# First modulation weight of a decoder layer taken in four slices of channels, with x and the weight rows between them

## What is computed

```python
mod = jax.nn.silu(c) @ w_ada[l] + b_ada[l]                        # (1, 6 * 1024)
sh1, sc1, g1, sh2, sc2, g2 = [m[:, None, :] for m in jnp.split(mod, 6, axis=-1)]
u = x * (1.0 + sc1) + sh1
proj = u @ w_in                                                   # q, k and v are 1536 of its columns
```

## Time and profile before

| | |
|---|---|
| median of 3 runs | 2779.15 us (2772.14 to 2779.37) |
| the profiled execution, its own time | 2779.9 us |
| its span | 2777.3 us |
| mean granted TensorE clock | 0.953 |
| TensorE busy with matmuls | 2509.4 us, 90% |
| VectorE, ScalarE, GpSimd busy | 53%, 40%, 30% |

### The profile page before, as it was taken

The page is one execution under the profiler, slowest core; times in us unless marked ns, Lnnn a source line. Parts: engine busy times, 40 slices in busy tenths (PEclk is TensorE's granted clock), DMA queues, the critical chain, the costliest instruction groups (busy, mean ns, idle before and its releaser), DMA issues. The chain is left out here.

```text
span 2777.3 us, 36162 instructions
## 1 busy us (share of the span) xinstructions
PE 2509.4 (90%) x12525; PEld 2093.1 (75%) x12526; DVE 1485.0 (53%) x1928; ACT 1114.9 (40%) x1819; POOL 829.5 (30%) x707
## 2 busy tenths in 40 slices
PE   5999899999999999999989969894998999999970
PEld 4788678778888888888878858774887888887850
DVE  6222155665665656665653356666547445526636
ACT  3122144554454545454530021112547546526633
POOL 2111022442222222222212235565232223222336
PEclk9999899999999999999999989996999999999985
DMA  7699666767666675766447546423558656627726
GB/s 260 236 315 321 239 211 185 247 199 233 193 213 185 212 216 177 218 211 198 156 152 247 167 153 229 144 99 122 166 154 286 179 151 189 202 62 224 252 68 242
DMA packets 258781, 549.61 MB, mean 198 GB/s; under 512 B 23860, under 2 KB 93608, under 8 KB 258024
## 3 DMA queue, kind: packets, MB, share of 16 engines
q1 hardware_dynamic: 236072, 483.07, 52.5%
q0 software_dynamic: 15248, 46.62, 7.6%
q10 hardware_dynamic: 7344, 18.35, 1.7%
HBM read 394.94 MB, written 153.02 MB: 197 GB/s over the span
## 5 line engine op out<-in xcount | busy, mean ns | idle before, releaser
L93 PE MATMUL mx_acc<-u_u,mx_w_hi 128*128 128x512 f32 x1792 | 572.8, 401 | 2.5 <-DMA mx_w_lo<-halves 2.5
L722 POOL TENSOR_TENSOR mx_wt<-mx_wt,mx_rest 128x127 f32<-128x127 f32 (+15 forms) x128 | 271.5, 2121 | 741.4 <-DVE mx_rest L924 741.4
L93 PEld LDWEIGHTS mx_acc<-u_u,mx_w_hi 128*128 128x128 f32 x1792 | 326.8, 190 | 68.2 <-DMA mx_w_lo<-halves 4.0
L932 DVE TENSOR_TENSOR mx_wt_lo<-mx_p_t,mx_wt_hi 128x512 fp32r<-128x512 f32 (+2 forms) x320 | 192.2, 605 | 331.2 <-ACT mx_wt_hi L887 329.4
L93 PE MATMUL mx_acc<-u_u,mx_w_lo 128*128 128x512 f32 x896 | 353.6, 395 | 0.0
L887 ACT ACTIVATE mx_wt_hi<-mx_p_t 128x512 fp32r<-128x512 f32 (+2 forms) x320 | 171.0, 534 | 408.5 <-PE mx_p_t L774 362.4
L924 DVE TENSOR_TENSOR_SCAN mx_rest<-mx_rest,mx_zero 128x128 f32<-128x128 f32 (+15 forms) x128 | 315.0, 2461 | 9.1 <-ACT mx_wt L869 9.1
L93 PE MATMUL moe_p_gu<-keep_wide_hi,moe_x_hi 128*128 128x512 f32 x656 | 262.6, 400 | 13.5 <-DVE keep_wide_lo L1916 13.0
L93 PE MATMUL moe_p_gu<-keep_wide_hi,moe_x_lo 128*128 128x512 f32 x656 | 257.8, 393 | 0.0
L93 PE MATMUL moe_p_gu<-keep_wide_lo,moe_x_hi 128*128 128x512 f32 x656 | 257.6, 393 | 0.0
L868 ACT ACTIVATE mx_rest<-mx_p_z 128x512 f32<-128x512 f32 (+2 forms) x320 | 171.1, 535 | 99.5 <-PE mx_p_z L761 59.2
(11 more groups left out here) (250 smaller groups left out, 5177.9 us busy)
## 6 DMA issues: line engine op xcount, KB each, us to landing
mx_w_hi<-halves SPq DMA_DIRECT2D x98, 512.0 KB, 3.8
mx_w_lo<-halves SPq DMA_DIRECT2D x98, 512.0 KB, 5.3
keep_stay<-in_w_gate SPq DMA_DIRECT2D x64, 512.0 KB, 5.2
keep_stay<-in_w_up SPq DMA_DIRECT2D x64, 512.0 KB, 6.2
keep_stay<-in_w_down SPq DMA_DIRECT2D x32, 1024.0 KB, 6.8
u_saved<-u_u SPq DMA_DIRECT2D x4, 4096.0 KB, 19.5
mx_w_mod<-in_w_ada SPq DMA_DIRECT2D x64, 256.0 KB, 5.2
gate_t<-mx_g_out SPq DMA_DIRECT2D x64, 256.0 KB, 5.2
```

The source lines that it names most:

```text
L93: mm = pe.matmul(out, a, b, start=first and n == 0, stop=last and n == len(pairs) - 1, skip_group_check=True)
L722: pool.tensor_tensor(wt[:, t % 2, 0:w - 1], wt[:, t % 2, 0:w - 1], rest[:, t % 2, 1:w], ALU.mult).then_inc(m["weights_done"], 1)
L932: dve.tensor_tensor(wt_lo[:, first:first + k - j], p_t[:, n % TR, 0:(k - j) * P].rearrange("p (j t) -> p j t", t=P), f32(wt_hi[:, first:fi ...
```

## The change

`w_ada` is no longer taken by halves but by four slices of channels: slice i holds the shift and the scale of channels 256 i to 256 i + 255, which is what u's row chunks k = 2i and 2i + 1 need. A slice is 2 MB, loaded by eight DMAs of 128 x 2 x 256 (rows of 1 KB, where they were 4 KB) into half of the second half of `stay`. SP's order becomes: slice 0, x, weight rows 0 and 1, slice 1, rows 2 and 3, slice 2, rows 4 and 5, slice 3, rows 6 to 15. Slice i waits until slice i - 2 has been summed up. VectorE sums a slice with one tensor_scalar and seven scalar_tensor_tensor of 512 channels, each of which waits for the one before it; TensorE then sums over partitions with four matmuls, and VectorE adds them to `mod`. ScalarE's affine of chunk k waits for its slice's step. These sums now stand inside the k loop, ahead of chunks 0, 2, 4 and 6. `p_t` has three buffers (a PSUM bank goes to `p_mod`). In the k loop TensorE's transposes of chunk k + 3 come behind the products of chunk k.

```diff
-    MW = FIRST_MOD * NB
-    AB, TR = 4, 4
+    AB, TR = 4, 3
-    MH, WH = MW // 2, QW // 2
+    WH = QW // 2
+    SLICES = 4
+    SC = D // SLICES
+    SK = KD // SLICES
...
-        ring = s.sb("ring", [P, RS, MH])
+        ring = s.sb("ring", [P, RS, D])
+        ada = flat(stay, 1).rearrange("p (b k h n) -> p b k h n", b=2, k=KD, h=2)
...
-            for n in range(2 * KD):
-                k, half = divmod(n, 2)
-
-                past(sp, m["summed"], n - RS + 1)
-                sp.dma_start(ring[:, n % RS], ada_view[:, k, half * MH:(half + 1) * MH]).then_inc(ring_in[n % RS], 16)
+
+            def load_slice(i):
+                past(sp, m["summed"], KD * (i - 1))
+                for q in range(SLICES):
+                    for h in range(2):
+                        sp.dma_start(ada[:, i % 2, SK * q:SK * (q + 1), h], ada_view[:, SK * q:SK * (q + 1), h * D + i * SC:h * D + (i + 1) * SC]
+                                     ).then_inc(ada_in[i % 2][q], 16)
+
+            def load_w(n):
+                half, k = divmod(n, KD)
+                past(sp, m["w_lo_done"], n - RS + 1)
+                sp.dma_start(ring[:, n % RS, 0:WH], in_view[:, k, c_q + half * WH:c_q + (half + 1) * WH]
+                             ).then_inc(ring_in[n % RS], 16)
+
+            load_slice(0)
             sp.dma_start(xr[:], x_view[:, 0]).then_inc(m["x_in"], 16)
             for n in range(2 * KD):
-                half, k = divmod(n, KD)
-                if n < RS:
-                    sp.wait_ge(m["summed"], 2 * KD - RS + n + 1)
-                else:
-                    sp.wait_ge(m["w_lo_done"], n - RS + 1)
-                sp.dma_start(ring[:, n % RS, 0:WH], in_view[:, k, c_q + half * WH:c_q + (half + 1) * WH]
-                             ).then_inc(ring_in[n % RS], 16)
+                if n < KD and n > 0 and n % SK == 0:
+                    load_slice(n // SK)
+                load_w(n)
...
-            for j in range(FIRST_COLS):
-                half, a = divmod(j * P, MH)
-                if a == 0:
-                    pe.wait_ge(m["summed"], 2 * KD - 1 + half)
-                mm = pe.matmul(p_mod[:, j:j + 1], msum[:, half, a:a + P], one[:], start=True, stop=True,
-                               skip_group_check=True)
-            mm.then_inc(m["mod_summed"], 1)
+            def sum_rows(i):
+                pe.wait_ge(m["summed"], KD * (i + 1))
+                for h in range(2):
+                    for j in range(SK):
+                        n = h * KD + i * SK + j
+                        mm = pe.matmul(p_mod[:, n:n + 1], msum[:, i, h, j * P:(j + 1) * P], one[:], start=True, stop=True,
+                                       skip_group_check=True)
+                mm.then_inc(m["mod_summed"], 1)
+
+            sum_rows(0)
             for k in range(TR):
                 turn(0, k)
             pe.wait_ge(m["cols_out"], 2)
             for k in range(KD):
+                pe.wait_ge(m["u_lo_done"], k + 1)
+                pe.wait_ge(m["w_lo_done"], k + 1)
+                for i in range(AB):
+                    part(0, i, k)
+                if (k + 1) % SK == 0 and k + 1 < KD:
+                    sum_rows((k + 1) // SK)
                 if TR + k < KD:
                     turn(0, TR + k)
-                pe.wait_ge(m["u_lo_done"], k + 1)
-                pe.wait_ge(m["w_lo_done"], k + 1)
-                if k == 0:
-                    pe.wait_ge(m["mod_step"], 1)
-                for i in range(AB):
-                    part(0, i, k)
...
-            act.wait_ge(m["mod_step"], 2)
             for k in range(KD):
+                act.wait_ge(m["mod_step"], k // SK + 2)
                 affine(0, k)
                 high_w(k)
...
+            def sum_slice(i):
+                for k in range(KD):
+                    dve.wait_ge(ada_in[i % 2][k // SK], 32 * (i // 2 + 1))
+                    if k == 0:
+                        ins = dve.tensor_scalar(msum[:, i], ada[:, i % 2, 0], csilu[:, 0:1], None, ALU.mult)
+                    else:
+                        dve.wait_ge(m["summed"], KD * i + k)
+                        ins = dve.scalar_tensor_tensor(out=msum[:, i], in0=ada[:, i % 2, k], scalar=csilu[:, k:k + 1],
+                                                       in1=msum[:, i], op0=ALU.mult, op1=ALU.add)
+                    ins.then_inc(m["summed"], 1)
+                dve.wait_ge(m["mod_summed"], i + 1)
+                dve.wait_ge(m["mod_step"], i + 1)
+                cols, sums = (v.rearrange("p (h k) -> p h k", h=2)[:, :, SK * i:SK * (i + 1)]
+                              for v in (mod[:, 0:FIRST_COLS], p_mod[:, 0:FIRST_COLS]))
+                dve.tensor_tensor(cols, cols, sums, ALU.add).then_inc(m["mod_step"], 1)
...
             for k in range(KD):
+                if k % SK == 0:
+                    sum_slice(k // SK)
                 high(0, k)
                 low_w(k)
```

More of the change, by code:

```diff
@@ L137, in load_piece, with front @@
             bass.ds(e, 1), :, a - KD:b - KD].rearrange("e p k d -> p (e k) d")).then_inc(piece_in[i], 16)
-def front(nc, used, keep, x, c, w_ada, b_ada, w_conv, w_in, u, u_in, u_saved, qk_hi, qk_lo, v_tok, halves):
+def front(nc, used, keep, stay, x, c, w_ada, b_ada, w_conv, w_in, u, u_in, u_saved, qk_hi, qk_lo, v_tok, halves):
     ident, mod, conv_cols, csilu, one = (keep[n] for n in ("ident", "mod", "conv_cols", "csilu", "one"))
     VR = NJ + KD + 3 * KC
-    MW = FIRST_MOD * NB
     QW, QKW = 3 * AW, 2 * AW
@@ L160, in front @@
         stage = s.sb("stage", [P, 2, 2 * NB])
-        acc, p_t = s.ps("acc", [P, AB, NB]), s.ps("p_t", [P, TR, NB])
-        p_vec, p_mod = acc[:, AB - 1, 0:VR], acc[:, AB - 2, 0:FIRST_COLS]
+        acc, p_t, p_mod = s.ps("acc", [P, AB, NB]), s.ps("p_t", [P, TR, NB]), s.ps("p_mod", [P, NB])
+        p_vec = acc[:, AB - 1, 0:VR]
         names = ("vec_in", "vec_turned", "ident_step", "silu_done", "cols_out", "summed", "mod_summed", "mod_step",
@@ L169, in front @@
         ring_in = [s.sem(f"ring_in{i}") for i in range(RS)]
+        ada_in = [[s.sem(f"ada_in{b}{i}") for i in range(SLICES)] for b in range(2)]
         block = ctx.enter_context(nc.Block())
-        msum = stage
+        msum = stage[:].rearrange("p a b -> p (a b)").rearrange("p (s h n) -> p s h n", s=SLICES, h=2)
         x_view = x.rearrange("b (g t p) d -> (b p) g t d", p=P, t=NB // P)
@@ L341, in high_w @@
                 half, k = divmod(n, KD)
-                act.wait_ge(ring_in[n % RS], 16 * (2 * KD // RS + n // RS + 1))
+                act.wait_ge(ring_in[n % RS], 16 * (n // RS + 1))
                 act.activation(w_hi[:, k, half * WH:(half + 1) * WH], ring[:, n % RS, 0:WH], ACT.Copy
                                ).then_inc(m["w_hi_done"], 1)
-            act.wait_ge(m["mod_step"], 2)
             for k in range(KD):
+                act.wait_ge(m["mod_step"], k // SK + 2)
                 affine(0, k)
@@ L377, in _ @@
             dve.tensor_copy(conv_cols[:], p_vec[:, NJ + KD:VR]).then_inc(m["cols_out"], 1)
[L378 to L387, removed]
             dve.wait_ge(m["cols_out"], 2)
-            dve.wait_ge(m["mod_summed"], 1)
-            dve.tensor_tensor(mod[:, 0:FIRST_COLS], mod[:, 0:FIRST_COLS], p_mod, ALU.add).then_inc(m["mod_step"], 1)
-            dve.wait_ge(m["mod_step"], 1)
             dve.tensor_scalar(mod[:, SC1:SC1 + KD], mod[:, SC1:SC1 + KD], 1.0, None, ALU.add).then_inc(m["mod_step"], 1)
+            def sum_slice(i):
[13 more added lines that the diff above has]
+                dve.tensor_tensor(cols, cols, sums, ALU.add).then_inc(m["mod_step"], 1)
             def high(tb, k):
@@ L2100, in hybrid_layer @@
         u_in = [Scope(nc, ctx, "u", used).sem(f"u_in{i}") for i in range(2)]
-        front(nc, used, keep, x, c, w_ada, b_ada, w_conv, w_in, u, u_in, u_saved, qk_hi, qk_lo, v_tok, halves)
+        front(nc, used, keep, stay, x, c, w_ada, b_ada, w_conv, w_in, u, u_in, u_saved, qk_hi, qk_lo, v_tok, halves)
         with ExitStack() as ectx:
```

## The result

| | before | changed |
|---|---|---|
| median | 2775.82 us (20 runs, 2770.41 to 2779.74) | 2783.38 us (20 runs, 2780.70 to 2789.21) |
| ratio, 95% interval | | 1.0030 (1.0023 to 1.0037) |
| span of the profiled execution | 2777.3 us | 2784.7 us |
| end of the first stage (start of its last eviction) | 327.7 us | 332.9 us |

The change makes the kernel slower by 7.6 us, 0.23% to 0.37%: right at the edge of the 0.3% that the prediction took as what can be told from no change. The forecast was +5.4 us, 2784.6 us, reckoned from the median of 3 runs of the kernel before (2779.15); over 20 runs that median is 2775.82.

The account below looks back on a forecast made before the run. Bound: SP's issue of the second x and the save, behind VectorE's low halves. T = 17.0 + 3 × 13.7 + 4.6 = 62.7 against 57.3, 5.4 us later, so 2784.6 us against the median 2779.15; range 2776 to 2797.

Parts of the forecast that it names:

- the second x and the save: SP's DMA issues of x's second block (2 MB) and the first u's store (4 MB), claimed to set the stage's end.
- T: Moment VectorE ends the eighth low half of the weight rows; forecast 62.7 us against 57.3 before, 5.4 us later.
- the second stop: TensorE's 3.58 us idle before 86.52, behind an eviction waiting for a qk_lo store; forecast to move to about 91.8.
- The first affine: ScalarE's first affine after x and four transposes; forecast start 17.0 us against 38.87, a head start of 21.9 us.
- The pair: VectorE's high, low_w, high, low_w for two k after each slice's step; forecast 4.6 us from the affine, as before.
- The seven scalar_tensor_tensor: VectorE's chained instructions in each slice's sum; forecast 0.77 us each, 5.4 us in all.
- The round trip: From a slice's sum through TensorE's four matmuls and VectorE's addition to the next affine; forecast 2.2 us.
- The period: Time between affines of successive pairs in the k loop; forecast 11.5 + 2.2 = 13.7 us, three times.
- TensorE's cover: TensorE, clock loss included, done 11.2 us after the affine, sum at 11.5; cost zero, cover 0.3 us.
- The rival in which TensorE becomes the bound: Low clock holds TensorE for whole pairs; period 19.3 us, +22 us in all, 2801 us; chance 0.10.
- The transfers: Rival: DMA transfers of slices and weight rows set the pace; T 6.8 us earlier, 2772 us; chance 0.10.
- The head start: Rival: stage bound by TensorE's start, so all 21.9 us are gained, 2757 us; chance 0.03.

Follow-up runs that it names:

- e2: Changed kernel with the save of the first u moved behind the stores of the fourth unit; +3.5 us against the kernel before (1.0003 to 1.0020).
- e3: Kernel before with the save of the first u moved behind the stores of the fourth unit; -3.1 us against the kernel before (0.9979 to 0.9996).
- e1: Changed kernel with the sums of slices 1 to 3 cut to one tensor_scalar each; +6.6 us against the kernel before (1.0013 to 1.0034).
- e7: Changed kernel with 12 unused matmuls ahead of the products of chunks 2, 4 and 6, two transpose buffers; +6.3 us against the kernel before.
- e10: Changed kernel measured again, unedited but for a comment; +5.9 us against the kernel before (1.0015 to 1.0033).
- e4: Kernel before with each of 16 w_ada loads made of two DMAs with 1 KB rows; +0.6 us against the kernel before (0.9992 to 1.0010).
- e5: Changed kernel with sums one slice ahead, slices 0 and 1 loaded and summed before x; +0.8 us against the kernel before (0.9991 to 1.0009).
- e6: e1 with 12 unused matmuls ahead of the products of chunks 2, 4 and 6, two transpose buffers; +0.4 us against the kernel before.

## Why the prediction was right

**The bound.** The prediction said that the stage's end hangs on the issue of the second x and the save, and that hangs on T. Measured: T later by 4.9 us, the issue by 5.5, the third eviction by 5.0, TensorE's second restart by 5.0, the end of the stage by 5.2. Forecast: 5.4 for all. e2 and e3 show that the wait behind the save is real. The profiles show T's hold on the stage. Of the eight that leave the save where it was, the four with T at 62.2 to 63.2 (changed, e1, e7, e10) end the stage at 331.8 to 334.9, and the four with T at 57.0 to 57.5 (before, e4, e5, e6) at 325.8 to 329.2. Not foreseen was how the shift is shared out: TensorE's first restart came 6.2 us later, for the last weight row landed late (ScalarE waited 2.03 us for it, until 73.12), and the second stop, 1.2 us shorter, gave that much back. TensorE's start, 21.3 us earlier (21.11 against 42.38), bought nothing.

**The sum, term by term.** The first affine: 17.0 forecast, 17.56 measured. The pair: 4.6 and 4.6. The held tensor_scalar: 1.5 and 1.50, so that it ended 6.0 us after the affine (6.1). The seven scalar_tensor_tensor: 5.4 forecast, and 5.9 measured. The mixer's two had 0.77 each; here seven take 0.84 each from first to last. The round trip: 2.2 forecast, and 1.3 measured (29.58 to 30.92). The error is in the price of the eight passes: 1.75 us from the earlier trace rows, 1.05 measured. The period is 12.0 + 1.3 = 13.35 instead of 11.5 + 2.2 = 13.7; the two errors offset each other. Three periods of 13.35 with 0.56 more at the start gave T = 62.2 instead of 62.7. That the sum came so near is in part luck, and so is the total: 2784.6 lies 1.2 us above the measured median, but it was reckoned from a median of the kernel before that was 3.3 us higher than that of 20 runs.

**TensorE's cover.** Its part of the pair was to end 11.2 us after the affine, with the clock's loss in it, and ended at 11.2 (28.75 less 17.56). The cover was called 0.3 us thick; it was 0.6 to 0.9, since the sums ran longer. The rival in which TensorE becomes the bound did not decide the changed kernel, and e7 shows that. But its mechanism was there: e1 ran at half clock for three stretches of 2 us and its periods were TensorE's. The price in the rival (19.3 us a period) was much too high. It counted the eight passes at 3.5 us, double a price that was already one at the low clock (1.87 us measured there, last section). And against the 6.0 us of a pair at full pace, one restart lost 1.8 us in the changed kernel (34.46 to 42.25) and 2.9 in e1, never a whole pair.

By the page TensorE: Matmul & The Clock Gate of the Trainium skill, section "HAM oscillation — how this bites in real kernels", each burst behind a wait can start at the low clock. The trace agrees: after each stop of 3.28 us two matmuls took 1.19 us where 0.70 is the full pace. The rival's 2801 us took more than that section states, a whole pair at the low clock, and the trace does not show it: at 38.18 two matmuls took 0.62 us again, and the pair went on until 42.24.

**The transfers** did not set the pace: the queues were nearly empty (12% busy) from 40 to 50 us. **The head start** was not kept. Both as argued. **The three transpose buffers** cost nothing: from 17.56 us to the end of the k loop ScalarE waits for no transpose.

**What is left.** The forecast has 5.4 us, the stage 5.2, the first median 7.6 and the second 5.9. In twelve profiled executions the rest of the program, which no kernel touched, took between 2441.0 and 2451.9 us, with no relation to the first stage. The 2.2 us by which the first pair of profiles differs there lies within this spread. Whether the changed kernel's later stages are truly 1 or 2 us longer, as the first interval would allow (its lower end is 6.4 us), was not settled; e4 only excludes the number and size of the early DMAs as a cause.

## What to carry to other kernels

Before an early start is counted as a gain, find what the end of the stage waits for and follow it back: here it was one DMA issue behind a chain on VectorE, and 21 us of head start on TensorE went into 26 us laid into that chain (T less the first affine: 44.7 us, 18.4 before). Work moved from ahead of a loop into it is free only on an engine that idles there; a round trip through a second engine idles it once more each time. And look at the order of a queue first: moving one 4 MB save and two evictions gave 7.8 us, where the slices, even one ahead, added nothing measurable.

## What the runs showed beyond that

The clock column can mislead at the start of a program, as it does here. From 22 to 24 us it says 1.00 in the changed kernel, but only six matmuls ran, as many as from 76 to 78 us at 0.50:

```profile
22.00:24.00 2.00, 2.00 (x6) 1.52 (x6) 1.90 (x3) 0.00 (x0) 1.31 (x1) 1.00 1.07 410
36.00:38.00 2.00, 2.00 (x7) 1.58 (x6) 1.79 (x3) 0.00 (x0) 0.66 (x1) 0.53 1.10 400
76.00:78.00 2.00, 2.00 (x6) 1.52 (x6) 0.15 (x1) 0.00 (x0) 0.00 (x0) 0.50 1.15 471
```

The eight passes of the first slice took 1.87 us and those of later slices 1.05; the 32 passes of the earlier trace rows took 0.22 each, which is the slow pace. That is why their price was too high. Before a price is taken from the beginning of a program, look at the matmuls themselves and not at the column alone: two of 512 columns in 1.19 us or in 0.70 tell the pace here.

And a filler pays only where its engine is the bound: twelve unused matmuls a period gave 6.2 us in e6 (against e1) and nothing clear of noise in e7 (1.3 us faster than the first measurement of the changed kernel, 0.4 slower than the second).
